# Square sums from a block of ones, root and reciprocal over 256 columns, and another order of ScalarE's copies, in a two-block transformer kernel on Trainium2

## The reference

```python
# first block
x = x + mx[:, :, 2] * yx                       # yx ends with @ w_out
h2 = modulate(rmsnorm(x, norm2_g), mx[:, :, 3], mx[:, :, 4])
x = x + mx[:, :, 5] * conv_ffn(h2, ffn_up, ..., ffn_down)
x = rmsnorm(x, final_g)
# second block
h = rms_norm(x, norm1_g);  p = h @ w_in        # q, k, v, gb, gc, hin, u
q, k = rms_norm(q), rms_norm(k)
y_attn = chunked_band_attention(q, k, v, rel_bias)   # softmax over 256 keys, then @ v
y_conv = gb * conv3(gc * hin);  y_pool = multiscale_pool(u)
x = x + concatenate([y_attn, y_conv, y_pool]) @ w_out
h2 = rms_norm(x, norm2_g)
x = x + square(relu(h2 @ w_mlp1)) @ w_mlp2
```

## Time and profile before

| | |
|---|---|
| median of 3 runs | 775.42 us (771.38 to 777.07) |
| the profiled execution | 777.96 us, its span 776.2 us |
| PE busy | 754.4 us, 97% of the span |
| DVE busy | 500.7 us, 65% |
| POOL busy | 399.4 us, 51% |
| ACT busy | 352.8 us, 45% |
| chain that ended last | PE 89%, DVE 4%, ACT 3%, POOL 2% |
| TensorE clock granted, mean | 0.989 |

### The profile page before, as it was taken

The page is one execution under the profiler, slowest core; times in us unless marked ns, Lnnn a source line. Parts: engine busy times, 40 slices in busy tenths (PEclk is TensorE's granted clock), DMA queues, the critical chain, the costliest instruction groups (busy, mean ns, idle before and its releaser), DMA issues.

```text
span 776.2 us, 14280 instructions
## 1 busy us (share of the span) xinstructions
PE 754.4 (97%) x5968; PEld 736.5 (95%) x5968; DVE 500.7 (65%) x908; ACT 352.8 (45%) x419; POOL 399.4 (51%) x215
## 2 busy tenths in 40 slices
PE   8996999999999998999999999999899999999998
PEld 5996889999999898999999999999899999999998
DVE  1687979475853647987766777366835655555563
ACT  5144432346445446555544547335554343334331
POOL 0145554365855995797888787765778300000000
PEclk9988999999999999999999999999999999999999
DMA  9854287813663454655545553534334555644511
GB/s 363 349 214 156 112 321 287 318 59 117 239 233 115 163 190 148 250 207 181 201 163 198 187 202 126 209 113 163 109 112 165 222 181 191 214 167 167 213 56 54
DMA packets 20804, 144.27 MB, mean 186 GB/s; under 512 B 2435, under 2 KB 2947, under 8 KB 3589
## 3 DMA queue, kind: packets, MB, share of 16 engines
q1 hardware_dynamic: 20592, 143.30, 50.5%
q10 hardware_dynamic: 148, 0.07, 0.0%
HBM read 142.31 MB, written 1.05 MB: 185 GB/s over the span
## 4 chain that ended last, share of the span: by engine, by line
PE 89%; DVE 4%; ACT 3%; POOL 2%; issue 1%; DMA 0%; DVEq 0%; ACTq 0%
PE bank L1358 23%; PE bank L1359 23%; PE bank L1360 22%; PE bank L1404 3%; PE bank L1376 3%; PE CP L1359 2%; PE CP L1358 2%; PE CP L1360 2%; POOL wlo L400 2%; PE bank L1466 2%; ACT whi L475 1%; PE bank L1416 1%; ACT SCR L718 1%; DVE GA L1048 1%; PE CP L1390 0%
## 5 line engine op out<-in xcount | busy, mean ns | idle before, releaser
L400 POOL TENSOR_TENSOR wlo<-raw,whi 128x512 fp32r<-128x512 f32 (+1 forms) x209 | 398.9, 1940 | 213.8 <-ACT whi L475 213.8
L475 ACT ACTIVATE whi<-raw 128x2048 fp32r<-128x2048 f32 x107 | 203.9, 1907 | 60.5 <-PE bank L1360 30.7
L1115 DVE SCALAR_TENSOR_TENSOR Y<-bank,vec,Y 128x189 f32<-128x189 f32 (+2 forms) x352 | 122.9, 421 | 39.7 <-ACT Y L659 39.5
L1358 PE MATMUL bank<-H2h,whi 128*128 128x256 f32 x352 | 99.0, 281 | 1.7 <-DVE H2l L1090 1.7
L1359 PE MATMUL bank<-H2l,whi 128*128 128x256 f32 x352 | 99.3, 282 | 0.0
L1360 PE MATMUL bank<-H2h,wlo 128*128 128x256 f32 x352 | 98.9, 281 | 0.0
L1358 PE MATMUL bank<-H1h,whi 128*128 128x256 f32 (+1 forms) x288 | 92.0, 319 | 1.5 <-issue 1.5
L400 DVE TENSOR_TENSOR wlo<-raw,whi 128x2048 fp32r<-128x2048 f32 (+1 forms) x32 | 70.4, 2200 | 35.8 <-ACT whi L475 35.8
L1359 PE MATMUL bank<-H1l,whi 128*128 128x256 f32 (+1 forms) x288 | 90.4, 314 | 0.0
L1360 PE MATMUL bank<-H1h,wlo 128*128 128x256 f32 (+1 forms) x288 | 90.2, 313 | 0.0
L1359 PE MATMUL bank<-H4l,whi 128*128 128x256 f32 x256 | 71.7, 280 | 0.0
(11 more groups left out here) (315 smaller groups left out, 1892.1 us busy)
## 6 DMA issues: line engine op xcount, KB each, us to landing
raw<-in_w_mlp SPq DMA_DIRECT2D x32, 1024.0 KB, 4.9
raw<-in_w_in SPq DMA_DIRECT2D x30, 1024.0 KB, 5.2
raw<-in_ffn_up SPq DMA_DIRECT2D x22, 1024.0 KB, 4.9
raw<-in_ada_hi SPq DMA_DIRECT2D x16, 1024.0 KB, 4.9
raw<-in_ffn_down SPq DMA_DIRECT2D x11, 1024.0 KB, 4.8
raw<-in_w_out SPq DMA_DIRECT2D x8, 1024.0 KB, 4.8
ada_p<-in_ada_p SPq DMA_DIRECT2D x4, 1024.0 KB, 14.1
ada_s<-in_ada_s SPq DMA_DIRECT2D x4, 1024.0 KB, 17.0
```

The costliest lines, as they stand in the source:

```text
L400: m = e.tensor_tensor(wlo[q % NHI][:, part], raw[place[split[q]] % NRAW][:, part], whi[q % NHI][:, part].bitcast(F32), ALU.subtract)
L475: e.activation(whi[q % NHI][:, :], raw[n % NRAW][:, :], ACT.Copy).then_inc(s["w_hi"], 1)
L1115: e.scalar_tensor_tensor(o[:, r0:r1, c0:c1], z[:, r0 + dr:r1 + dr, c0 + dc:c1 + dc], cw[:, f, tap:tap + 1], o[:, r0:r1, c0:c1], ALU.mult, ...
L1358: e.matmul(out, h[:, col:col + P], xh, start=first, stop=False, skip_group_check=True)
```

## The change

Four edits:

1. The sums of squares behind w_out and w_out_2 are made with a 128 x 128 block of ones as the stationary operand and the squares (256 columns) as the moving one. The result has every token's sum on all 128 partitions at once. ScalarE takes the root of 128 x 256 in place in PSUM (`root_rows`), VectorE the reciprocal of 128 x 256: behind w_out in place in PSUM, behind w_out_2 into RR. The `rows` products and the copy to RR of the kernel before are gone.
2. Job col1 now holds the row from which VectorE reads, so its table entry says that its bank is free at h2_mul 8. Jobs row1 and rows3 are gone; col3 is free at rr_done 3.
3. The waits on row_x are renumbered.
4. ScalarE makes the high part of w_out_2 tile 1 and copies the second half of the transposed probabilities ahead of its wait for the convolution.

```diff
-MISC += [(f"rdo_row{n}", "rdo_gain", 2 * n + 2) for n in range(2)] + [("col1", "rms_x", 1)]
+MISC += [(f"rdo_row{n}", "rdo_gain", 2 * n + 2) for n in range(2)] + [("col1", "h2_mul", 8)]
...
-MISC2 += [(f"av{n}", "mix_lo", n + 3) for n in range(2)] + [("col3", "rms_x", 2), ("rows3", "rr_done", 3)]
+MISC2 += [(f"av{n}", "mix_lo", n + 3) for n in range(2)] + [("col3", "rr_done", 3)]
...
-    where["row1"], before["row1"] = 3, ("qf", 10)
...
+        def root_rows(b):
+            e.activation(b, b, ACT.Sqrt, bias=eps[:, 0:1], scale=1.0 / D).then_inc(s["rms_x"], 1)
+
         e.wait_ge(s["col_x"], 1)
-        root(misc_bank["col1"], 2, D, 0, "rms_x")
+        root_rows(bank[misc_bank["col1"]][:, 0:T])
...
         turn_probabilities(0)
+        high(turn["w_in_2", 9] + 2)
+        turn_probabilities(1)
         e.wait_ge(s["conv_2"], 8)
         e.activation(MXh[:, 4:6, :], YC[:, :, :], ACT.Copy).then_inc(s["mix_hi"], 1)
-        high(turn["w_in_2", 9] + 2)
-        turn_probabilities(1)
...
         e.wait_ge(s["col_x"], 2)
-        root(misc_bank["col3"], 2, D, 0, "rms_x")
-        e.wait_ge(s["row_x"], 3)
-        e.activation(RR[:, :], bank[misc_bank["rows3"]][:, 0:T], ACT.Copy).then_inc(s["rr_done"], 1)
+        root_rows(bank[misc_bank["col3"]][:, 0:T])
...
         project("w_out", 0, "x1", SQ1, "sq1", "sq1_sum", lambda ks: None)
-        reciprocal(2, 0, ("rms_x", 1), "rstd_x")
-        e.wait_ge(s["row_x"], 1)
+        r1 = bank[misc_bank["col1"]][:, 0:T]
+        e.wait_ge(s["rms_x"], 1)
+        e.reciprocal(r1, r1).then_inc(s["rstd_x"], 1)
+        e.wait_ge(s["rstd_x"], 1)
...
-        reciprocal(2, 0, ("rms_x", 2), "rstd_x")
+        e.wait_ge(s["rms_x"], 2)
+        e.reciprocal(RR[:, :], bank[misc_bank["col3"]][:, 0:T]).then_inc(s["rr_done"], 1)
...
-        def square_columns(b, sq, f, n):
+        def square_sums(b, sq, f, n):
             for k in range(f, f + n):
-                for t in range(2):
-                    m = e.matmul(b[:, t:t + 1], sq[:, k, t * P:(t + 1) * P], ones[:, 0:1], start=k + t == 0,
-                                 stop=k == KT - 1, skip_group_check=True)
+                m = e.matmul(b[:, 0:T], ones[:, 0:P], sq[:, k, :], start=k == 0, stop=k == KT - 1)
             return m
...
         m.then_inc(s["col_x"], 1)
-        b = misc("row1")
-        e.wait_ge(s["rstd_x"], 1)
-        rows(b, [wide(0), wide(1)], "row_x")
...
-                if i == 0:
-                    b = misc("rows3")
-                    e.wait_ge(s["rstd_x"], 2)
-                    rows(b, [wide(0), wide(1)], "row_x")
```

More of the change, by code:

```diff
@@ L698, in scalar @@
         high(turn["w_in_2", 1] + 2)
-        e.wait_ge(s["row_x"], 2)
+        e.wait_ge(s["row_x"], 1)
         b = bank[misc_bank["rows2"]]
@@ L1093, in vector @@
         for k in range(KT):
-            e.scalar_tensor_tensor(TMP1[:, k, :], XR[:, k, :], A2[:, k:k + 1], bank[misc_bank["row1"]][:, 0:T],
+            e.scalar_tensor_tensor(TMP1[:, k, :], XR[:, k, :], A2[:, k:k + 1], r1,
                                    ALU.mult, ALU.mult).then_inc(s["h2_mul"], 1)
@@ L1625, in tensor @@
         e.wait_ge(s["sq1_sum"], 2)
-        square_columns(bs, SQ1, 0, 2)
+        square_sums(bs, SQ1, 0, 2)
         for j in range(2):
             e.wait_ge(s["sq1"], 4 + j)
-            m = square_columns(bs, SQ1, 6 + j, 1)
+            m = square_sums(bs, SQ1, 6 + j, 1)
         m.then_inc(s["col_x"], 1)
-        b = misc("row1")
-        e.wait_ge(s["rstd_x"], 1)
-        rows(b, [wide(0), wide(1)], "row_x")
         def h2_ready(k):
@@ L1785, in tensor @@
         e.wait_ge(s["sq3_sum"], 2)
-        square_columns(bs, SQ3, 0, 2)
+        square_sums(bs, SQ3, 0, 2)
         def h4_ready(k):
@@ L1794, in finish_norm @@
                 e.wait_ge(s["sq3"], 4 + j)
-                m = square_columns(bs, SQ3, 6 + j, 1)
+                m = square_sums(bs, SQ3, 6 + j, 1)
             m.then_inc(s["col_x"], 1)
```

## The result

The changed kernel takes 787.77 us (median of 4 runs, 781.46 to 791.51) against 775.57 us before (median of 4, one run more than stood ahead of the prediction): 12.2 us more. The ratio of the runs is 1.0133, 95% interval 1.0096 to 1.0170, so slower by 1.0 to 1.7%. The profiled execution is the quickest of the four, 781.46 us with a span of 779.7.

A forecast was written before the change was run, and what follows sets the result against it. TensorE, busy 754.4 of 776.2 us, was taken as the bound. The terms 5.2 + 0 - 0.4 + 3.0 + 1.6 = +9.4 us, against the 775.42 us median, gave 784.8 us, range 778.5 to 789.5.

The forecast's parts named there:

- Edit 1: Behind w_out: 256-column root and reciprocal replace the path over TensorE; first TMP product +0.9 us later, reciprocal 1.77 us.
- Edit 2: Ahead of ffn_up: TensorE waits for h2_mul 8; +5.2 us, of which 4.3 from the table entry; half clock behind valued 0.
- Edit 4: Behind w_in_2: GpSimd's pieces run beside VectorE's end of the convolution; TensorE starts +3.0 us later, half clock +1.6 us.
- Edit 3: Norm behind w_out_2: four row passes leave TensorE's unbroken stream, -0.36 us, called sure; root and reciprocal covered by w_mlp1.
- The clock: Half clock behind w_in_2: absent after the 2.93 us pause, expected after the longer 5.9 us one; +1.6 us, between 0 and +2.5.
- A: Rival: behind w_in_2 GpSimd's pieces do not hold VectorE up, no half clock; +3.9 us, 779.3 us; chance 0.15.
- B: Rival: behind w_in_2 VectorE and GpSimd collide but no half clock follows; +7.8 us, 783.2 us; chance 0.18.
- C: Rival: TensorE's late start at ffn_up is given back by slack in the stage; +4.2 us, 779.6 us; chance 0.07.
- D: Rival: half-clock stretches grow, +1.0 us behind w_out and +0.9 behind w_in_2; +11.3 us, 786.7 us; chance 0.10.
- E: Rival: reciprocal as quick as a plain product, wait on h2_mul free, no collision behind w_in_2; 773.7 us; chance 0.02.

The follow-up runs named there:

- late_wait: Changed kernel, with TensorE's wait for the ffn_down banks moved from ahead of ffn_up to just ahead of the first ffn_down products; ratio 1.0116 against the kernel before.
- b_copies: Kernel before, with ScalarE's last probability copies ahead of its convolution wait, the high part of w_out_2 tile 1 left behind the copy of YC; ratio 0.9998.
- pool_hold: Changed kernel, with GpSimd holding the low part of w_out_2 tile 1 until the convolution and its low part are done; ratio 1.0102 against the kernel before.
- b_edit3: Kernel before, with only the norm behind w_out_2 changed (block of ones, 256-column root and reciprocal, no row products); ratio 1.0050.
- act_back: Changed kernel, with ScalarE's old order behind w_in_2 (copy of YC, high part, probability copies); ratio 1.0133 against the kernel before.
- e3_hold: Kernel before with the changed norm behind w_out_2, VectorE holding its w_mlp2 tile 1 low part until GpSimd's w_mlp1 tile 3 is done; ratio 0.9984.
- all_mended: Changed kernel with the ffn_down wait moved later, the w_out_2 tile 1 high part back behind the copy of YC, and VectorE's hold; ratio 1.0009 against the kernel before.
- best2: Kernel before with the changed norm behind w_out_2, VectorE's hold and the probability copies ahead, w_out untouched; 776.03 us against 777.30, ratio 0.9975.
- b_edit12: Kernel before, with only the sums, root and reciprocal behind w_out, the table entry and the renumbered waits changed; ratio 1.0104.
- e3_pad: Kernel before with the changed norm behind w_out_2, plus two unread products at the removed row products' old place; one run, 775.62 us.
- b_edit4: Kernel before, with only ScalarE's new order behind w_in_2 (high part and probability copies ahead of the convolution wait); ratio 1.0043.

## Why the prediction was right, and where it was not

784.8 us with 778.5 to 789.5 was forecast, 787.77 measured; of the +9.4 us forecast, +12.2 came by the medians and +10.3 by the ratio.

- *Edit 1.* The reciprocal of 256 columns takes 1767 ns, behind w_out_2 1758; the slope of two short rows had given 1.77. The Trainium skill (VectorE: DVE Perf Modes, "First, the fixed hardware budget") gives a repeat count of 8; the estimate made from it by reading this as eight cycles a column was 0.4 us too high. Root 0.45 in place of 0.39. From the last w_out product to the first TMP it is 1.0 us more, forecast 0.9.
- *Edit 2.* Forecast 5.2 us with edit 1, measured 5.5, of which late_wait shows 4.5 to be the early wait. The clock behind it was valued at 0. Column B is 0.5 to 1.0 us above the kernel before in the four kernels with this pause (189.5 to 190.0); but b_copies, with w_out untouched, has 189.7 and late_wait, with the wait moved, 190.1, so it isn't shown that this belongs to the pause.
- *Edit 4.* The mechanism was right, the size a little off: C grew by 2.3 us against 3.0. The last two convolution steps took 1.4 to 1.5 us each as forecast, and the product of YC 1.63 in place of 0.69; the low part of YC met only the end of a piece, 0.98 in place of 1.5. The gain of 0.9 without the collision is there in b_copies and pool_hold. The half clock came and cost 1.6 in D, as forecast for the changed kernel.
- *Edit 3.* This step failed. "-0.36 us, sure, since the stream is unbroken there" held up to the next tiles and missed what an earlier TensorE does 18 us later. I had looked at who is late, never at who is early. The term was +3.9 us by b_edit3's ratio. Column E has 2.0 us of it in b_edit3, all of it the wait, and 3.6 in late_wait, act_back and pool_hold, where a stretch of half clock stood behind the wait. With the collision mended the term was 0 and not -0.36 (e3_hold, all_mended, best2). The rows for it were in the kernel before: VectorE's low part, 2.5 us long, starts 5.6 us behind GpSimd's start on w_mlp1 tile 3, and TensorE comes to that tile 0.3 us after it is done.
- *The clock.* That 2.93 us behind w_in_2 are not enough for half clock was read from one execution. act_back, b_edit12 and e3_hold had it behind the same wait. b_edit3 and e3_pad, with the same wait, did not. So it cannot be booked to the longer pause of edit 4 alone: edits 1 and 2 alone, and edit 4 alone, each lost it in their profiles, and in the changed kernel it comes once. That may be one reason why the parts alone, 8.1 + 3.3 + 3.9 = 15.3 us, add up to more than the whole; it is argued and not tested.
- *The number.* That 9.4 and the measured 10.3 to 12.2 us lie so close is partly luck. In columns A to D of the changed kernel's profile 9.9 us came (5.5, 0.5, 2.3 and 1.6), against 9.8 forecast without edit 3. Edit 3's loss stood on top of that, and what kept the sum down was at least one run, the profiled one, with a shorter step of TensorE, which nobody had forecast.
- *The rivals.* A (no collision) is refuted by the rows of the changed kernel and b_edit4, 1.63 us for the product of YC; b_edit4's time alone, +3.3 us against the 3 that were to decide, would not have settled it. B is refuted by the clock rows of the profiled execution. C (given back): column B grew, nothing came back. D's longer half clock may have been there behind w_out (column B, above), and was not behind w_in_2. E is refuted: the reciprocal took 1.77 us and the wait 4.5.

## What to carry to other kernels

Where a semaphore table stands for a buffer, look where the wait for it is issued: the entry was right for the bank and five tiles too early in TensorE's stream, and cost over four times what the longer reciprocal did. A wait that an engine loses lets its neighbour run on; before moving one, ask what the freed engine will now run beside. And a stream without pauses is not safe against a gain: 0.4 us earlier turned the order of two engines that hold each other up, and one explicit wait repaired it. It gained nothing either, since the tile that TensorE came to early was done only just in time.

## What the runs showed of the hardware that I had not expected

TensorE's step from product to product has two values at the same granted clock of 1.00. Stretches of equal length with TensorE busy throughout (length, busy us of PE, clock, DMA share, GB/s): the changed kernel's first, then b_edit4's.

```profile
310.00:460.00 150.00, 150.00 (x1275) 1.00 0.54 190
630.00:760.00 130.00, 130.00 (x1149) 1.00 0.50 178
```

```profile
310.00:460.00 150.00, 149.96 (x1324) 1.00 0.57 205
630.00:760.00 130.00, 130.00 (x1106) 1.00 0.45 161
```

Products of the same kinds come every 118 ns (150 us by 1275, 130 by 1106) or every 113 (130 by 1149, 150 by 1324). In b_edit4's profile that made column B 183.1 us and not 189.0, in the changed kernel's column E 178.3 and not the 184.2 of b_edit3, which has the same wait and no half clock either. In both the shorter step began behind a pause of TensorE, and in b_edit4 it had ended by the stage behind w_out_2. What chooses it stays open. It comes to 3% of a stage, so columns can be compared only where the step is the same, and with 5.9 us it accounts for most of the distance of the profiled execution from the median of the changed kernel's runs.
